# Queries and keys of the differential heads by products of 512 columns, their halves added afterwards

## The chip, the cores and the metric

The kernel runs on one core of a Trainium2 chip. The metric is the device time of one execution in microseconds; 1415.09 us is the median of 3 runs of the kernel before.

## The reference, cut to what matters

The reference is two transformer blocks over 256 tokens of width 1024. The first block normalizes its input, multiplies it by one wide matrix, and splits the result between an RWKV-7 mixer, a differential attention and a gate. The queries and keys of the differential attention are the columns 1792 to 2815 of that product. Cut to them:

```
h = rmsnorm(x, norm_mix_g)                       # (256, 1024)
u = h @ w_in                                     # all projections
q, k, v = split(u_attn, 3)                       # 512 columns each
q = q.reshape(S, 4, 2, 64) * 64 ** -0.5          # factor 0.125
k = k.reshape(S, 4, 2, 64)
s = einsum('qhcd,khcd->hcqk', q, k) - slope * dist, causal
pr = softmax(s);  attn = pr[:, 0] - lam * pr[:, 1];  o = attn @ v
```

## The kernel before, in words

Every projection is computed to full precision from two parts of each factor. The normalized input, still without its factor per token, is held as a high part HH and a low part HL, side by side in one array `h2` (8 slices of 128 features, the two parts, 256 tokens). A weight piece of 2048 columns per partition is loaded (`raw`), ScalarE casts it to its high part (`hi`, L2649), and VectorE subtracts to get the low part (`lo`, L3017). The product is hi·HH + hi·HL + lo·HH, summed in a PSUM bank of 512 columns. Three pieces are in flight, each with its own buffers of `raw`, `hi` and `lo`, and a piece's `hi` is written once TensorE is done with the piece three before it.

The weights of the first block come in pieces of 256 features: seven for the RWKV columns, then four for the queries and keys (columns 1792, 2048, 2304 and 2560; called pieces 1 to 4 here), then the values in wider pieces. Each of the four is a `cols_piece`: for each of two groups of 128 features and each of 8 slices it issues three products of 256 columns (`mm3`, L2131 to L2133), 48 in all, into one bank, one half of the bank for each group. When the bank is full, one VectorE operation multiplies the 512 columns by the factor per token (`RB2`) and, for queries, by 0.125, and writes them to `qT` (L3359) or `kTt` (L3362). That frees the bank.

In the same stretch the RWKV mixer runs: many small products of 64 rows by 64 columns in plain float32 (L2378, L2393), each of which waits for VectorE or ScalarE to have taken the one before from its bank. A planner (`weave`) lays these chains and the wide projections, which it calls fill, into one order for each engine. It keeps estimated times for each engine and always emits the step that could start first; of a `cols_piece` it may break off after every two slices, 0.72 us by its costs. The order is fixed when the program is built. Each engine works through its own list in order, and semaphores hold an instruction until its data is there (`bank_full`, `hi_ready`, `lo_ready`) or its bank is free (`bank_free`). Banks go from a pool of 8, in the order in which they were given back.

The up and gate projections of the later layers already use another form, `wide_runs`: two banks, one for each group of 128 features; a product of 512 columns multiplies `hi` by HH and HL at once (L2219), and one of 256 columns adds lo·HH to the first half of the bank (L2226). That is 16 products of 512 and 16 of 256 columns in one unbroken step. Of such a bank the two halves have to be added afterwards: ScalarE copies the second half out (L2846), and VectorE adds the first half to it (L2987). Every second `wide_runs` begins with one slice of `hi`, then all of `lo`, then the rest of `hi`.

Of the kernel before, what the change touches and what calls it, by code (L numbers as in the profile page):

```python
# [10 lines left out]
ALU = mybir.AluOpType  # L11
# [21 lines left out]
LEAD = 10.0  # L33
# [187 lines left out]
def program(nc, ws, xin, pin, colsin, constin, smallin, rowin, out):  # L221
# [4 lines left out]
    with ExitStack() as ctx:  # L226
# [28 lines left out]
        rstd_ready = Sig(sem("rstd_ready"))  # L255
        factors = Sig(sem("token_factors"))
        diag_ready = Sig(sem("diag_ready"))
        c_part = Sig(sem("c_part"))
        c_ready = Sig(sem("c_ready"))
        rwkv_a = Named(sem("rwkv_act"))  # L260
# [278 lines left out]
        script = []  # L539
# [1063 lines left out]
                state["gates"] = True  # L1603

        def diff():
            while "vd" not in state or "bonus" not in state:
                yield None
            yield "dve"
            emit("lam", dve=0.5, act=0.2, us=state["bonus"], v=diff_v.add(), v_a=diff_a.add())
# [52 lines left out]
                state["ob_v"] = diff_v.n  # L1662
            state["ob"] = pv

        to_shift = []
        early = []

# [14 lines left out]
        def mixers_fill(nm):  # L1682
            for p, c in enumerate(RWKV_ORDER):
                def shift(sl, c, nxt, p=p):
                    early.append((p, c, sl, cur[0]))
                    if p == 1:
                        nm.rows()
                    if p:
                        to_shift.extend(early)
                        early.clear()  # L1690
                    if nxt:
                        emit_lo(nxt)
                    return True
                if p == 0:
                    yield from first_piece(c, nm.h_needs, shift)
                else:
                    yield from cols_piece("w_in", 0, c, "h", nm.h_needs, shift)

            def dq(sl, c, nxt):
                emit("dqk", dve=0.7, slot=sl, n=(c - 1792) // 128)  # L1700
                if nxt:
                    emit_lo(nxt)
                state["dk"] = sl

            for c in range(1792, 2816, 256):
                yield from cols_piece("w_in", 0, c, "h", nm.h_needs, dq)

            def vd(sl, b, h):
                emit("d_v", act=0.7, slot=sl, b=b, rstd=nm.rstd)
                state["dv"] = sl  # L1710

            yield from rows_mat("w_in", 0, 8, 2816, 512, "h", nm.h_needs, vd)
            state["vd"] = True

            def gate_in(g, half):
                def evac(sl, b, h):
                    emit("gate_in", dve=0.7, slot=sl, g=g, b=b, half=half, rstd=nm.rstd)
                    if b:
                        state["g" + g, half] = sl
                return evac  # L1720

            for g, c in (("A", 3328), ("B", 4352)):
                yield "pe"
                while g == "B" and ("fold", 1) not in state:
                    yield None
                for half in range(2):
                    yield from rows_mat("w_in", 0, 8, c + 512 * half, 512, "h", nm.h_needs, gate_in(g, half))
            yield "pe"
            while "ob" not in state or "gates" not in state:
                yield None  # L1730

            def pb(half):
                def evac(sl, b, h):
                    emit("pb", dve=0.7, slot=sl, b=b, half=half, sig=state["sig", "B", half])
                return evac

            for half in range(2):
                if half:

                    yield "pe"  # L1740
                    while "oa" not in state:
                        yield None
                yield from rows_mat("w_proj_b", 0, 4, 512 * half, 512, "ob", lambda k, b: (diff_v.sem, state["ob_v"]),
                                    pb(half))

        weave([shifts(), rwkv_decays(), rwkv_keys(), (rwkv_chain(), LEAD), (rwkv_block(0), LEAD), (rwkv_block(1), LEAD),
               (rwkv_out(0), LEAD), (rwkv_out(1), LEAD), (diff(), LEAD + 2.0), gates()],
              [mixers_fill(nm)])

# [362 lines left out]
        def tensor_program(e):  # L2112
# [27 lines left out]
            for s in script:  # L2140
# [351 lines left out]
                elif kind == "d_soft":  # L2492
# [1 line left out]
                    for z in s["slots"]:  # L2494
                        claim(z)
                    if h == 0:
                        read_out(state["dk"])
                    for a0, a1 in ((0, 128), (128, 384)):
                        for c, z in enumerate(s["slots"]):
                            t = e.matmul(banks[z.b][:, a0:a1], qT[half(c), h, a0:a0 + 128], kTt[half(c), h, 0:a1 - a0],  # L2500
# [97 lines left out]
                elif kind == "pv":  # L2598
# [8 lines left out]
                                         ETb[s["i"]][:, p, c0:c0 + 256 - q0], start=b == 0, stop=b == 1)  # L2607
                    t.then_inc(full[sl.b], 1)

        def scalar_program(e):  # L2610
            own = [0]

# [25 lines left out]
            for s in script:  # L2638
# [51 lines left out]
                                 accum_out=st[:, i:i + 1]).then_inc(x_squared.sem, 1)  # L2690


                elif kind == "shift_old":
                    read_out(sl)
                    c, u_ = s["c"] // 128, ub[s["i"]]
# [253 lines left out]
        def vector_program(e):  # L2949
# [25 lines left out]
            def row_top(sl, bias, E, top):  # L2975
# [2 lines left out]
                                       top[:, 0:1])  # L2978
                return e.tensor_tensor_reduce(E[:, 128:384], banks[sl.b][:, 128:384], bias[:, 128:384], 1.0, LOWEST,
                                              ALU.add, ALU.max, top[:, 1:2])  # L2980

            def add_halves(s, to):

# [39 lines left out]
            for s in script:  # L3023
# [330 lines left out]
                    e.tensor_tensor(obL[:, h, :], oT[:, :], obH[:, h, :].bitcast(F), ALU.subtract).then_inc(diff_v.sem, 1)  # L3354
                elif kind == "dqk":
                    n = s["n"]
                    ready(sl)
                    if n < 4:
                        e.scalar_tensor_tensor(qT[:, n:n + 2, :], b2(sl), 0.125, RB2, ALU.mult,  # L3359
                                               ALU.mult).then_inc(free[sl.b], 1)  # L3360
                    else:
                        e.tensor_tensor(kTt[:, n - 4:n - 2, :], b2(sl), RB2, ALU.mult).then_inc(free[sl.b], 1)  # L3362


                elif kind == "gate_in":
                    b, o = s["b"], slice(512 * s["half"], 512 * s["half"] + 512)
                    e.wait_ge(rstd_ready.sem, s["rstd"])
# [369 lines left out]
```

## Time and profile before

| | |
|---|---|
| median of 3 runs | 1415.09 us (1414.96 to 1415.43) |
| profiled execution | 1415.34 us, of which the span is 1413.4 us |
| TensorE busy | 1406.8 us of the span |
| VectorE, ScalarE busy | 1179.5 us, 819.2 us |
| pieces 1 to 4 begin | about 56.4 us after the span's start |

The profile gives for each group of instructions its line, engine, operation, operands, number, busy time, mean duration of one, and the idle time before them. A matmul's duration in it is longer than the distance to the next one, since matmuls are pipelined: what one costs is read from the start of one to the start of the next. A matmul in plain float32 shows as two records.

### The profile page before, as it was taken

What the parts mean: (1) busy time and instruction counts of PE and PEld (TensorE: products, weight loads), DVE (VectorE), ACT (ScalarE), POOL (GpSimd) and SP (SyncE); (2) the same over time, 40 slices, a digit from 0 to 9 for tenths busy, and PEclk for the clock granted to TensorE, in tenths of its full rate; (3) what the DMA queues carried; (4) which work ended last, traced back from release to release, by engine and by line L of the source; (5) the groups of instructions that cost most, each with busy time, mean ns of one, the idle gap of its engine ahead of it and who ended that gap; (6) DMA issues with size and microseconds to landing.
All of it is one profiled execution on the core that took longest, in us unless ns stands there. A gap on an engine that the chain in (4) does not pass through costs nothing.

```text
span 1413.4 us, 22918 instructions
## 1 busy us (share of the span) xinstructions
PE 1406.8 (100%) x9197; PEld 1197.1 (85%) x9197; DVE 1179.5 (83%) x1641; ACT 819.2 (58%) x1103; POOL 26.5 (2%) x93
## 2 busy tenths in 40 slices
PE   9999999999999999999999999999999999999999
PEld 8988778888888888889878888888888887888887
DVE  6876786898877898998868988988889798688897
ACT  7735474565447555555766665555555557665562
POOL 0000000000001100000000000000000000000000
PEclk9999999999999999999999999999999999999999
DMA  8441236555554555455434555545555453355543
GB/s 335 155 151 62 101 110 208 173 185 203 194 221 179 185 203 185 173 208 192 141 118 172 185 195 187 213 169 197 200 179 197 165 177 148 112 201 195 180 177 119
DMA packets 36105, 249.12 MB, mean 176 GB/s; under 512 B 4128, under 2 KB 4256, under 8 KB 6688
## 3 DMA queue, kind: packets, MB, share of 16 engines
q1 hardware_dynamic: 35712, 247.46, 49.4%
q8 instruction: 74, 1.21, 0.4%
q14 instruction: 31, 0.25, 0.1%
q10 hardware_dynamic: 288, 0.19, 0.1%
HBM read 246.59 MB, written 1.05 MB: 175 GB/s over the span
## 4 chain that ended last, share of the span: by engine, by line
PE 97%; DMA 1%; ACT 1%; DVE 0%; issue 0%; SPq 0%; DVEq 0%; ACTq 0%
PE ps L2219 24%; PE ps L2131 16%; PE ps L2133 15%; PE ps L2132 15%; PE ps L2226 13%; PE ps L2393 2%; PE ps L2203 1%; PE ps L2207 1%; PE ps L2209 1%; DMA raw<-ws 1%; PE ps L2307 1%; PE ps L2606 1%; PE ps L2586 1%; PE ps L2595 1%; PE ps L2378 0%; ACT hi L2649 0%
## 5 line engine op out<-in xcount | busy, mean ns | idle before, releaser
L3017 DVE TENSOR_TENSOR lo<-raw,hi 128x2048 fp32r<-128x2048 f32 (+1 forms) x230 | 525.0, 2283 | 60.3 <-ACT hi L2649 57.6
L2649 ACT CAST hi<-raw 128x2048 fp32r<-128x2048 f32 (+1 forms) x230 | 439.8, 1913 | 186.6 <-PE ps L2133 118.9
L2219 PE MATMUL ps<-h,hi 128*128 128x512 f32 x1504 | 359.0, 390 | 0.0
L2219 PEld LDWEIGHTS ps<-h,hi 128*128 128x128 f32 x1504 | 276.4, 188 | 52.5
L2131 PE MATMUL ps<-hi,a 128*128 128x512 f32 x516 | 205.0, 397 | 0.0
L2133 PE MATMUL ps<-hi,a 128*128 128x512 f32 x516 | 201.4, 390 | 0.0
L2132 PE MATMUL ps<-lo,a 128*128 128x512 f32 x516 | 201.2, 390 | 0.0
L2226 PEld LDWEIGHTS ps<-h,lo 128*128 128x128 f32 x1504 | 192.2, 190 | 7.9
L2226 PE MATMUL ps<-h,lo 128*128 128x256 f32 x1504 | 194.4, 282 | 0.0
L2846 ACT COPY a<-ps 128x256 f32<-128x256 f32 x208 | 76.1, 373 | 143.5 <-PE ps L2219 78.5
L2131 PEld LDWEIGHTS ps<-hi,a 128*128 128x128 f32 x516 | 96.9, 188 | 22.6 <-issue 2.4
L2133 PEld LDWEIGHTS ps<-hi,a 128*128 128x128 f32 x516 | 96.9, 188 | 20.9
L2132 PEld LDWEIGHTS ps<-lo,a 128*128 128x128 f32 x516 | 97.0, 188 | 19.1
L2131 PE MATMUL ps<-hi,h 128*128 128x512 f32 x272 | 112.0, 412 | 0.0
L2133 PE MATMUL ps<-hi,h 128*128 128x512 f32 x272 | 106.3, 391 | 0.0
L2132 PE MATMUL ps<-lo,h 128*128 128x512 f32 x272 | 106.2, 390 | 0.0
L2987 DVE TENSOR_TENSOR a<-ps,a 128x256 f32<-128x256 f32 x208 | 81.9, 420 | 17.0 <-ACT a L2846 15.1
L2131 PE MATMUL ps<-h,hi 128*128 128x256 f32 x224 | 64.8, 289 | 0.9 <-DVE lo L3017 0.9
L2132 PE MATMUL ps<-h,hi 128*128 128x256 f32 x224 | 63.4, 283 | 0.0
L2133 PE MATMUL ps<-h,lo 128*128 128x256 f32 x224 | 63.4, 283 | 0.0
L2131 PEld LDWEIGHTS ps<-hi,h 128*128 128x128 f32 x272 | 51.1, 188 | 12.2 <-issue 2.3
L2133 PEld LDWEIGHTS ps<-hi,h 128*128 128x128 f32 x272 | 51.0, 188 | 11.2
(383 smaller groups left out, 1800.1 us busy)
## 6 DMA issues: line engine op xcount, KB each, us to landing
raw<-ws SPq DMA_DIRECT2D x229, 1024.0 KB, 4.8
X<-xin SPq DMA_DIRECT2D x8, 256.0 KB, 5.3
raw<-ws SPq DMA_DIRECT2D x2, 512.0 KB, 6.5
out<-X SPq DMA_DIRECT2D x4, 256.0 KB, 2.2
small<-small SPq DMA_DIRECT2D x1, 992.5 KB, 12.8
const<-const SPq DMA_DIRECT2D x1, 900.0 KB, 6.8
a<-row SPq DMA_DIRECT2D x1, 512.0 KB, 6.2
const<-const SPq DMA_DIRECT2D x1, 388.0 KB, 13.2
```

The lines of the kernel that those rows point to most:

```text
L2131: e.matmul(o, ah, bh, start=start, stop=False)
L2132: e.matmul(o, ah, bl, start=False, stop=False)
L2133: return e.matmul(o, al, bh, start=False, stop=stop)
L2203: t = e.matmul(b2(sl), wh[:, k, a:a + 128], h2[:, k, :, :], start=k == 0, stop=False)
L2207: t = e.matmul(b2(sl)[:, 0, :], wl[:, k, a:a + 128], HH[:, k, :], start=False, stop=hi_first and k == 7)
L2219: t = e.matmul(b2(s["slots"][u]), wh[:, k, 128 * u:128 * u + 128], h2[:, k, :, :], start=k == 0, stop=last)
L2226: t = e.matmul(b2(s["slots"][u])[:, 0, :], wl[:, k, 128 * u:128 * u + 128], HH[:, k, :], start=False, stop=last)
L2393: t = e.matmul(banks[z.b][half(q ^ n), 64 * h:64 * h + 64], TB[blk][l][half(q), h, :], TB[blk][r][half(q), h, :], start=True, stop=True)
L2649: e.copy(hi[j % NSPL][:, n], raw[j % NRAW][:, n]).then_inc(hi_ready, 1)
L2846: e.copy(half_to[s["to"]][s["j"]][:, s["u"], :], b2(sl)[:, 1, :]).then_inc(half_a.sem, 1)
L2987: e.tensor_tensor(to[:, u, :], b2(x)[:, 0, :], half_to[kind][j][:, u, :], ALU.add).then_inc(free[x.b], 1)
L3017: e.tensor_tensor(lo[j % NSPL][:, n], raw[j % NRAW][:, n], hi[j % NSPL][:, n].bitcast(F), ALU.subtract).then_inc(lo_ready, 1)
```

## The change

The four pieces become `wide_runs`. A new chain in the planner, `queries`, takes the two banks of each piece in turn: a step `halves` on ScalarE copies the second half of both banks into the place in `qT` or `kTt` (two copies of 256 columns), and a step `dqk` on VectorE adds the first half of each (two operations of 256 columns, each of which frees its bank), waits for its own writing, and then multiplies the 512 columns in place by the factor per token (and 0.125). The heads' first score product waits for the last of these. The chain `diff` starts only when `queries` has ended, besides what it waited for before.

```
 def queries():
+    for n in range(4):
+        while len(to_scale) <= n:
+            yield None
+        c, sl, other, at = to_scale[n]
+        yield "act", at
+        emit("halves", act=0.7, slots=(other, sl), qk="dq" if n < 2 else "dk", n=2 * n % 4, v=[half_a.add() for _ in range(2)])
+        halves = script[-1]["v"]
+        yield "dve"
+        emit("dqk", dve=1.4, slots=(other, sl), halves=halves, n=(c - 1792) // 128, v=scaled_v.add())
+        for x in (other, sl):
+            give(x)
+    state["dk"] = scaled_v.n
...
-            def dq(sl, c, nxt):
-                emit("dqk", dve=0.7, slot=sl, n=(c - 1792) // 128)
-                if nxt:
-                    emit_lo(nxt)
-                state["dk"] = sl
+            def dq(sl, c, nxt, other):
+                to_scale.append((c, sl, other, cur[0]))
+                emit_lo(nxt)
+                return True
...
-                yield from cols_piece("w_in", 0, c, "h", nm.h_needs, dq)
+                yield from wide_runs("w_in", 0, c, nm.h_needs, begin, dq)
...
-                        read_out(state["dk"])
+                        e.wait_ge(scaled_v.sem, state["dk"])
...
+                elif kind == "halves":
+                    to = halves_of(s)
+                    for u, x in enumerate(s["slots"]):
+                        ready(x)
+                        e.copy(to[:, u, :], b2(x)[:, 1, :]).then_inc(half_a.sem, 1)
...
+            def meet_halves(s, to):
+                for u, x in enumerate(s["slots"]):
+                    e.wait_ge(half_a.sem, s["halves"][u])
+                    e.tensor_tensor(to[:, u, :], b2(x)[:, 0, :], to[:, u, :], ALU.add).then_inc(free[x.b], 1)
+                for x in s["slots"]:
+                    read_out(x)
+                return to
...
-                    ready(sl)
-                    if n < 4:
-                        e.scalar_tensor_tensor(qT[:, n:n + 2, :], b2(sl), 0.125, RB2, ALU.mult,
-                                               ALU.mult).then_inc(free[sl.b], 1)
-                    else:
-                        e.tensor_tensor(kTt[:, n - 4:n - 2, :], b2(sl), RB2, ALU.mult).then_inc(free[sl.b], 1)
+                    t = meet_halves(s, halves_of({"qk": "dq" if n < 4 else "dk", "n": n % 4}))
+                    t = e.scalar_tensor_tensor(t, t, 0.125 if n < 4 else 1.0, RB2, ALU.mult, ALU.mult)
+                    t.then_inc(scaled_v.sem, 1)
```

The lines move with the edit: what was L2131 to L2133 is L2151 to L2153 in the changed kernel, L2219 and L2226 are L2239 and L2246, the small products L2378 and L2393 are L2398 and L2413, and the cast L2649 is L2673.

On TensorE, around the first score product of the mixer (a_70 by a_71, 64x64), stood before, in the middle of piece 3:

```order
L2131 MATMUL ps<-h,hi_52 128x256
L2132 MATMUL ps<-h,hi_52 128x256
L2133 MATMUL ps<-h,lo_55 128x256
L2378 MATMUL ps<-a_70,a_71 64x64 [waits rwkv_dve,bank_free3,bank_free2]
L2378 MATMUL ps<-a_70,a_71 64x64 x15
L2131 MATMUL ps<-h,hi_52 128x256
L2132 MATMUL ps<-h,hi_52 128x256
L2133 MATMUL ps<-h,lo_55 128x256
```

It now stands between pieces 3 and 4, the second score product behind piece 4:

```order
L2246 MATMUL ps<-h,lo_55 128x256 [waits lo_ready]
L2246 MATMUL ps<-h,lo_55 128x256 x15
L2398 MATMUL ps<-a_70,a_71 64x64 [waits rwkv_dve,bank_free4,bank_free6]
L2398 MATMUL ps<-a_70,a_71 64x64 x15
L2239 MATMUL ps<-h,hi_53 128x512 [waits hi_ready,bank_free0,bank_free7]
L2239 MATMUL ps<-h,hi_53 128x512
L2246 MATMUL ps<-h,lo_56 128x256 [waits lo_ready]
L2246 MATMUL ps<-h,lo_56 128x256 x15
L2239 MATMUL ps<-h,hi_53 128x512 x14
L2398 MATMUL ps<-a_71,a_70 64x64 [waits rwkv_dve,bank_free4,bank_free6]
L2398 MATMUL ps<-a_71,a_70 64x64 x15
```

A piece is no longer broken into, and the small products that lay in four places inside pieces 3 and 4 come between or behind them, closer together. Some rows on, they follow one another through the two banks 4 and 6 (the third score product, then the turning of the values with L2370, between them a chain product L2413), with one to three slices of the value projection between:

```order
L2398 MATMUL ps<-a_70,a_71 64x64 [waits rwkv_dve,bank_free4,bank_free6]
L2398 MATMUL ps<-a_70,a_71 64x64 x15
L2151 MATMUL ps<-hi_54,h 128x512
L2152 MATMUL ps<-lo_57,h 128x512
L2153 MATMUL ps<-hi_54,h 128x512
L2370 MATMUL ps<-const,a_67 128x128 [waits c_ready,bank_free6]
L2370 MATMUL ps<-const,a_67 128x128 x3
L2413 MATMUL ps<-a_86,a_85 64x64 [waits bank_free4]
L2413 MATMUL ps<-a_86,a_85 64x64 x15
L2370 MATMUL ps<-const,a_67 128x128 [waits c_ready,bank_free6]
L2370 MATMUL ps<-const,a_67 128x128 x3
L2151 MATMUL ps<-hi_54,h 128x512 [waits bank_free2,lo_ready]
```

What moved here is the distance: fewer slices of the projection lie between small products that use the same two banks.

On VectorE stood before, from the second query piece (a_101 is `qT`, a_102 is `kTt`) on:

```order
L3359 SCALAR_TENSOR_TENSOR a_101<-ps,RB 128x512 [waits bank_full7]
L3152 SCALAR_TENSOR_TENSOR a_67<-a_69,cols,a_67 128x256 [waits c_part]
L3153 SCALAR_TENSOR_TENSOR a_67<-a_69,cols,a_67 128x256
L3219 TENSOR_TENSOR a_85<-ps,const 128x256 [waits bank_full2,rwkv_dve]
L3219 TENSOR_TENSOR a_85<-ps,const 128x256 [waits bank_full3]
L3017 TENSOR_TENSOR lo_56<-raw_50,hi_53 128x2048 [waits hi_ready,bank_free2]
L3219 TENSOR_TENSOR a_86<-ps,const 128x256 [waits bank_full5,rwkv_dve]
L3219 TENSOR_TENSOR a_87<-ps,const 128x256
L3219 TENSOR_TENSOR a_86<-ps,const 128x256 [waits bank_full6]
L3219 TENSOR_TENSOR a_87<-ps,const 128x256
L3362 TENSOR_TENSOR a_102<-ps,RB 128x512 [waits bank_full1,bank_free5]
L3228 TENSOR_TENSOR a_90<-a_85,const 128x512 [waits bank_free3]
```

and now, from the taking of the first score product on (a_85), up to that of the second (a_86, a_87):

```order
L3257 TENSOR_TENSOR a_85<-ps,const 128x256 [waits bank_full6,rwkv_dve]
L3257 TENSOR_TENSOR a_85<-ps,const 128x256 [waits bank_full4]
L3055 TENSOR_TENSOR lo_57<-raw_51,hi_54 128x2048 [waits hi_ready,bank_free6]
L3015 TENSOR_TENSOR a_101<-ps,a_101 128x256 [waits half_act] x2
L3396 SCALAR_TENSOR_TENSOR a_101<-a_101,RB 128x512 [waits bank_free2,bank_free1]
L3234 TENSOR_TENSOR a_70<-a_67,a_77 128x8x128 [waits rwkv_act,c_ready]
L3235 TENSOR_TENSOR st<-a_77,st 128x4x3
L3240 SCALAR_TENSOR_TENSOR a_80<-a_67,cols 128x256 [waits rwkv_dve]
L3240 SCALAR_TENSOR_TENSOR a_80<-a_67,cols 128x256 x3
L3257 TENSOR_TENSOR a_86<-ps,const 128x256 [waits bank_full6,rwkv_dve]
L3257 TENSOR_TENSOR a_87<-ps,const 128x256
L3257 TENSOR_TENSOR a_86<-ps,const 128x256 [waits bank_full4]
```

One operation per piece has become three, and the second score product is now taken behind the second piece's three and behind four other operations of the mixer.

On ScalarE stood before, between two casts of weights and behind them:

```order
L2649 CAST hi_52<-raw_49 128x2048 [waits bank_full1,raw_in0]
L2696 ACTIVATE a_67<-a_68,st 128x256 [waits bank_free0]
L2697 ACTIVATE a_67<-a_68,st 128x256
L2755 COPY a_88<-ps 128x512 [waits bank_full7]
L2755 COPY a_89<-ps 128x512 [waits bank_full2]
L2649 CAST hi_53<-raw_50 128x2048 [waits bank_full4,raw_in1]
L2747 COPY a_74<-ps 128x512 [waits bank_full0]
```

and now, with the copies of pieces 3 and 4:

```order
L2721 COPY a_102<-ps 128x256 [waits bank_full3]
L2721 COPY a_102<-ps 128x256 [waits bank_full5]
L2673 CAST hi_53<-raw_50 128x2048 [waits bank_full0,raw_in1]
L2776 COPY a_74<-ps 128x512 [waits bank_full6] x2
L2721 COPY a_102<-ps 128x256 [waits bank_full7]
L2721 COPY a_102<-ps 128x256 [waits bank_full0]
L2784 COPY a_88<-ps 128x512 [waits bank_full4]
L2784 COPY a_89<-ps 128x512 [waits bank_full6]
```

The copies of piece 4 stand behind the two that take the turned values (a_74) out of bank 6.

## Rows read from the trace of the kernel before

**Rows 1.** The page: busy time of each engine, granted clock by slices
```profile
PE 1406.8 (100%) x9197; PEld 1197.1 (85%) x9197; DVE 1179.5 (83%) x1641; ACT 819.2 (58%) x1103; POOL 26.5 (2%) x93
...
PEclk9999999999999999999999999999999999999999
```

**Rows 2.** Stretches: us, busy us of PE, PEld, DVE, ACT, POOL; clock, DMA, GB/s
```profile
60.00:80.00 20.00, 20.00 (x252) 19.26 (x252) 16.57 (x20) 7.45 (x7) 0.00 (x0) 1.00 0.30 107
80.00:100.00 20.00, 20.00 (x239) 16.27 (x237) 16.42 (x23) 7.84 (x9) 0.00 (x0) 1.00 0.53 187
```

**Rows 3.** Timeline of TensorE (start, us, what): first products of pieces 1 and 2
```profile
56.37 0.28 PE L2131 MATMUL ps<-h,hi 128*128 128x256 f32 x1
...
62.13 0.28 PE L2131 MATMUL ps<-h,hi 128*128 128x256 f32 x1
```

**Rows 4.** Timeline of TensorE: a piece by `wide_runs` in a later layer
```profile
269.83 4.92 PE L2219 MATMUL ps<-h,hi 128*128 128x512 f32 x21
274.59 2.08 PE L2226 MATMUL ps<-h,lo 128*128 128x256 f32 x16
276.50 0.63 PE L2219 MATMUL ps<-h,hi 128*128 128x512 f32 x2
```

**Rows 5.** Timeline of TensorE: small products inside the projections
```profile
69.21 0.28 PE L2133 MATMUL ps<-h,lo 128*128 128x256 f32 x1
69.42 0.69 PE L2378 MATMUL ps<-a,a 64*64 64x64 f32 x32
70.05 0.39 PE L2131 MATMUL ps<-h,hi 128*128 128x256 f32 x1
70.27 0.28 PE L2132 MATMUL ps<-h,hi 128*128 128x256 f32 x1
...
90.11 1.13 PE L2357 MATMUL ps<-a,const 128*128 128x256 f32 x4
90.89 0.58 PE L2131 MATMUL ps<-hi,h 128*128 128x512 f32 x1
...
93.85 1.03 PE L2357 MATMUL ps<-a,const 128*128 128x256 f32 x4
94.81 1.15 PE L2393 MATMUL ps<-a,a 64*64 64x64 f32 x32
...
99.89 1.16 PE L2393 MATMUL ps<-a,a 64*64 64x64 f32 x64
```

**Rows 6.** Timeline of VectorE over pieces 2 to 4
```profile
62.33 0.69 DVE L3359 SCALAR_TENSOR_TENSOR a<-ps,RB 128x512 f32<-128x512 f32 x1 [2.83 <-PE ps L2133]
...
69.39 0.48 DVE L3152 SCALAR_TENSOR_TENSOR a<-a,cols,a 128x256 f32<-128x256 f32 x1
...
70.24 0.76 DVE L3219 TENSOR_TENSOR a<-ps,const 128x256 f32<-128x256 f32 x2
70.91 2.28 DVE L3017 TENSOR_TENSOR lo<-raw,hi 128x2048 fp32r<-128x2048 f32 x1
73.11 1.41 DVE L3219 TENSOR_TENSOR a<-ps,const 128x256 f32<-128x256 f32 x4
...
76.16 0.68 DVE L3228 TENSOR_TENSOR a<-a,const 128x512 f32<-128x512 f32 x1
...
80.69 1.22 DVE L3196 TENSOR_TENSOR a<-a,a 128x1024 f32<-128x1024 f32 x1
...
82.03 1.68 DVE L3202 SCALAR_TENSOR_TENSOR a<-a,cols 128x256 f32<-128x256 f32 x4
```

**Rows 7.** The page: groups of copies and additions of halves in later layers
```profile
L2846 ACT COPY a<-ps 128x256 f32<-128x256 f32 x208 | 76.1, 373 | 143.5 <-PE ps L2219 78.5
...
L2987 DVE TENSOR_TENSOR a<-ps,a 128x256 f32<-128x256 f32 x208 | 81.9, 420 | 17.0 <-ACT a L2846 15.1
```

**Rows 8.** Groups by line, 260 to 400 us, VectorE: scaling from and to SBUF
```profile
L3396 DVE SCALAR_TENSOR_TENSOR a<-a 128x512 f32<-128x512 f32 x16 | 11.1, 693 | 1.7
```

**Rows 9.** Timeline of ScalarE: copies of the turned values
```profile
86.37 0.59 ACT L2747 COPY a<-ps 128x512 f32<-128x512 f32 x1 [0.62 <-PE ps L2350]
```

More of the change, by code:

```diff
@@ L257, in program @@
         diag_ready = Sig(sem("diag_ready"))
+        scaled_v = Sig(sem("queries_scaled"))
         c_part = Sig(sem("c_part"))
@@ L1605, in diff @@
         def diff():
-            while "vd" not in state or "bonus" not in state:
+            while "vd" not in state or "bonus" not in state or "dk" not in state:
                 yield None
@@ L1663, in diff, with queries @@
             state["ob"] = pv
+        to_scale = []
+        def queries():
+            for n in range(4):
[10 more added lines that the diff above has]
+            state["dk"] = scaled_v.n
         to_shift = []
@@ L1697, in mixers_fill, with begin @@
                     yield from cols_piece("w_in", 0, c, "h", nm.h_needs, shift)
-            def dq(sl, c, nxt):
-                emit("dqk", dve=0.7, slot=sl, n=(c - 1792) // 128)
-                if nxt:
-                    emit_lo(nxt)
-                state["dk"] = sl
+            def dq(sl, c, nxt, other):
+                to_scale.append((c, sl, other, cur[0]))
+                emit_lo(nxt)
+                return True
+            def begin(sl, c, u):
+                pass
             for c in range(1792, 2816, 256):
-                yield from cols_piece("w_in", 0, c, "h", nm.h_needs, dq)
+                yield from wide_runs("w_in", 0, c, nm.h_needs, begin, dq)
             def vd(sl, b, h):
@@ L1744, in mixers_fill @@
                                     pb(half))
-        weave([shifts(), rwkv_decays(), rwkv_keys(), (rwkv_chain(), LEAD), (rwkv_block(0), LEAD), (rwkv_block(1), LEAD),
+        weave([shifts(), queries(), rwkv_decays(), rwkv_keys(), (rwkv_chain(), LEAD), (rwkv_block(0), LEAD), (rwkv_block(1), LEAD),
                (rwkv_out(0), LEAD), (rwkv_out(1), LEAD), (diff(), LEAD + 2.0), gates()],
@@ L2608, in tensor_program, with halves_of @@
                     t.then_inc(full[sl.b], 1)
+        def halves_of(s):
+            return {"dq": qT, "dk": kTt}[s["qk"]][:, s["n"]:s["n"] + 2, :]
         def scalar_program(e):
```

## The prediction

> **What bounds the kernel now.** I read the page first, then the stretches, then TensorE's own timeline, and only then the lists of VectorE and ScalarE. On the page TensorE is busy for 1406.8 of 1413.4 us at a granted clock of 0.9 or more in every slice [rows 1], and from 60 to 100 us, where the four pieces lie, it is busy for all of both stretches, at clock 1.00, which is the level of 2.4 GHz [rows 2]. VectorE is busy there for 16.6 and 16.4 of 20 us, ScalarE for less than 8 [rows 2]. A pipelined TensorE that shows as busy can still lose time, so the reader should look at the starts: piece 1 begins at 56.37 us and piece 2 at 62.13 us [rows 3], 48 products in 5.76 us, 0.120 us each, with nothing lost between them. In this part, then, the end of the program moves by exactly what TensorE's list loses or gains. VectorE waits for it (2.83 us for the end of piece 1 [rows 6]), not the reverse.
>
> **The change part by part.** *The products.* A slice of one group cost three products of 256 columns, 0.360 us. In a later layer 21 products of 512 columns take from 269.83 to 274.59 us, 0.2267 us each, and 16 of 256 take from there to 276.50 us, 0.119 us each [rows 4]. A slice will cost 0.346 us, a piece 16 x 0.346 = 5.54 us instead of 5.76 us. Four pieces save 4 x 0.22 = 0.88 us. The columns streamed are the same, 768 for a slice; what goes is what a product costs beyond its columns: 256 columns more cost 0.2267 - 0.120 = 0.107 us, so each product carries about 0.013 us besides, and 64 products disappear.
>
> The Trainium skill puts this besides-cost lower: TensorE: Matmul & The Clock Gate, section "Back-to-back issue gap", gives a gap of the columns divided by 2.4 GHz plus 2.5 ns. By it the four pieces would save 64 x 2.5 ns = 0.16 us; an estimate from that page, and the trace of this kernel does not agree with it (0.120 us for 256 columns, where the page would have 0.109 us). The sum goes by the rows.
>
> *The small products.* A score product inside a piece costs more than its own time: the product before it takes 0.21 us instead of 0.12 us to its successor, the first one after it 0.22 us instead of 0.12 us [rows 5]; and with an estimated 0.1 us to let the 64x64 block end, one entry and exit is near 0.30 us. Between the start of piece 1 and the first paired chain product (both mixer blocks interleaved) the order has ten such blocks before and seven now, which saves up to 3 x 0.30 = 0.90 us. But inside the merged blocks the shape changes six times instead of three, and such a change costs 0.1 to 0.2 us: 128-row products followed by the projection last 0.78 us (90.11 to 90.89), followed by 64x64 products 0.96 us (93.85 to 94.81) [rows 5]. Three more at 0.15 us take 0.45 us back. I take a saving of 0.45 us, between 0 and 0.90 us.
>
> *VectorE.* Before: four operations of 0.69 us [rows 6], 2.8 us. Now per piece two additions of 0.42 us [rows 7] and one scaling of 0.69 us from SBUF [rows 8], 1.53 us; 6.1 us for four, 3.4 us more. The stretches leave 7 us of VectorE idle between 60 and 100 us [rows 2], and the wait of 2.83 us for piece 1 disappears because the next weight split no longer stands behind the scaling. So most of it is hidden. It is not hidden in one place. By the new order VectorE takes the first score product when piece 3 and that product are done: pieces 1 to 3 end at 56.37 + 3 x 5.54 = 72.99 us, the product about 0.8 us later, its results are read from 73.9 us on. Then follow, before TensorE's third score product can have its two banks: the two takings (0.67 us, 70.24 to 70.91), the split (2.20 us, 70.91 to 73.11) [rows 6], piece 2's additions and scaling with a wait for its own writing (1.4 us from one start to the next), three operations of the mixer (1.34 us, 80.69 to 82.03, then 1.7 us), and the four takings of the second score product (1.41 us) [rows 6]: 8.7 us, so 82.6 us. TensorE, which does piece 4 (5.54 us), the second score product (0.8 us) and three slices of the values (9 x 0.2267 = 2.04 us) in that time, is there at 82.3 us. It loses 0.4 us. The next product, the turning of the values, needs the first bank of the third score product; in between VectorE has two operations of 0.48 us and one of 0.68 us and a taking of 0.42 us [rows 6], until about 84.4 us, against one slice on TensorE until 84.2 us: 0.2 us more. Then the second turning's bank is freed by a ScalarE copy of 0.59 us [rows 9], with one slice (0.68 us) beside it: 0.1 to 0.2 us. Together I take 0.8 us of new waiting, between 0 and 2.5 us: none if VectorE's operations overlap a little better than start to start, 2.5 us if each of its nine operations of pieces 1 to 3 brings 0.2 us of semaphore time with it (1.8 us).
>
> *ScalarE.* Eight copies of 0.37 us [rows 7], 3.0 us, on an engine with 12 us idle in each of the two stretches. The copies of piece 4 stand between the turned values and the outputs of the first chain products; these outputs are late by 0.7 us, and what waits for their banks comes a score product later, so I cost it at nothing; without that cover it would be 0.7 us, inside the bound above.
>
> *What else moves.* The first 512-column products of a piece wait only for the cast and no longer for the split; no wait for a split was seen here, so nothing is gained. A piece holds two banks instead of one; the last two it takes are free 2 us ahead by the same walk. From the first paired chain product on, the orders of all engines are the same but for bank numbers, and VectorE and ScalarE wait for TensorE there in both. DMA queues keep their order.
>
> *The sum.* -0.88 - 0.45 + 0.8 = -0.5 us on the profiled execution of 1415.34 us: 1414.8 us. That execution is 0.25 us above the median of 1415.09 us, so the median I predict is 1414.5 us.
>
> **The rivals.** *A. No new waiting.* The walk along VectorE's list is accurate to a few tenths only, and its first margin is 0.4 us. For it: VectorE gains 2.8 us on its list at piece 1. Against it: the additions stand right before the operations that the second score product waits behind. Time: 1415.09 - 0.88 - 0.45 = 1413.8 us.
>
> *B. The two shared banks decide.* The third score product, the turning of the values and the chain products between go through the banks 4 and 6 one right after the other, and every one of them waits for VectorE or ScalarE to empty the bank. TensorE's distance between them is one to three slices, VectorE's up to 8.7 us. From 1.3 us of waiting on, this eats the whole saving; at the upper bound of 2.5 us the time is 1415.09 - 1.33 + 2.5 = 1416.3 us. If ScalarE's late outputs also hold TensorE, 0.7 us more: 1417.0 us. For it: VectorE's list is filled to 82 percent here already [rows 2]. Against it: after the first paired chain product both lists meet TensorE again, so no delay is passed on.
>
> *C. The saving per product is not there*, because a 512-column product inside the mixer's stretch meets the small ones: with the low bound of all (no gain from the blocks, 0.16 us for the products) and 0.8 us of waiting the time would be 1415.7 us. Against it: the same form holds its 0.2267 us in a later layer [rows 4].
>
> **How the numbers follow.** Forecast (0 to 1.2 us of waiting, saved 0.9 to 1.7 us): 0.60, own range 1413.6 to 1415.3 us. A: 0.15. B: 0.18. C: 0.07. The range that should hold 8 in 10 goes from the full saving of 1.78 us without waiting (1413.3 us) to B without the ScalarE part (1416.3 us); with the runs' spread of half a microsecond I take 1413.0 to 1416.4 us. A run of this kernel tells 0.2 percent, 2.8 us, from no change. Faster by that would need 1412.3 us or less, more than all savings together: 0.04. Slower by it would need 1417.9 us or more, over 4 us of waiting: 0.06. The rest, 0.90, lies within.
>
> **What the changed profile would show.** Starts of pieces 1 and 2 5.54 us apart; the products of 512 and 256 columns at 0.227 and 0.120 us. VectorE's wait of 2.8 us at piece 1 gone. TensorE idle some tenths before the third score product and before the first turning of the values, and nowhere else new up to 100 us; the first paired chain product (99.89 us before [rows 5]) starts at about 99.3 us, and everything behind it half a microsecond early. I am wrong if that product starts later than before, if TensorE waits at piece 4 for its banks, or if anything behind it moves by more than what stands there.

## The result and the profile after

The changed kernel takes 1418.34 us (median of 13 runs, 1417.09 to 1419.58) where the kernel before takes 1415.23 us (13 runs beside them, 1414.93 to 1416.07): 3.1 us more, a ratio of 1.0022 with a 95% interval of 1.0014 to 1.0030. The prediction was 1414.5 us with a range of 1413.0 to 1416.4 us, so it was wrong, and it had given such a slowdown a chance of 0.06. The profiled execution of after has a span of 1416.6 us (1418.44 us by its own time), 3.2 us above that of before.

The page gives no hint of the place: the busy time of TensorE even fell, and the clock is the same, to be held beside [rows 1].

```profile
PE 1406.4 (99%) x9133; PEld 1193.2 (84%) x9133; DVE 1182.0 (83%) x1649; ACT 819.6 (58%) x1111; POOL 26.6 (2%) x93
...
PEclk9999999999999999999999999999999999999999
```

The stretches do (columns as in [rows 2]). Where the four pieces lie, TensorE now lacks 0.27 us. The holes are behind them, in stretches whose code the change does not touch: 0.73 us between 100 and 120 us and 2.12 us between 140 and 160 us, where before was busy for all of the 20 us.

```profile
60.00:80.00 20.00, 20.00 (x148) 17.47 (x147) 17.42 (x20) 8.88 (x13) 0.00 (x0) 1.00 0.36 127
80.00:100.00 20.00, 19.73 (x296) 15.42 (x299) 18.20 (x31) 8.96 (x12) 0.00 (x0) 1.00 0.46 163
100.00:120.00 20.00, 19.27 (x449) 15.96 (x444) 9.39 (x30) 10.80 (x24) 0.00 (x0) 1.00 0.16 58
...
140.00:160.00 20.00, 17.88 (x400) 13.99 (x399) 10.53 (x25) 11.51 (x25) 0.00 (x0) 1.00 0.16 55
```

Now the parts in order. TensorE's timeline of after, the answer to [rows 3, 4]: piece 1 starts at 56.80 us, and after 16 products of 512 and 16 of 256 columns piece 2 starts at 62.36 us. That is 5.56 us for a piece instead of 5.76 us, and 0.228 and 0.119 us for a product.

```profile
56.80 3.82 PE L2239 MATMUL ps<-h,hi 128*128 128x512 f32 x16
60.45 2.08 PE L2246 MATMUL ps<-h,lo 128*128 128x256 f32 x16
62.36 0.63 PE L2239 MATMUL ps<-h,hi 128*128 128x512 f32 x2
```

The small products of after, the answer to [rows 5]: the third score product (83.15 us, with a wait in front of it), the first turning of the values (84.83 us), and the first paired chain product at 99.80 us. Counted from the start of piece 1, that product comes after 43.00 us; before it came after 99.89 - 56.37 = 43.52 us. So up to here the change gains 0.52 us. The very next paired product, at 101.79 us, is cut in two: 56 products, a hole, 8 products. In before the same one was a whole run of 64.

```profile
83.15 0.69 PE L2398 MATMUL ps<-a,a 64*64 64x64 f32 x32 [0.19 <-issue]
...
84.83 0.66 PE L2370 MATMUL ps<-const,a 128*128 128x128 f32 x4
...
99.80 1.16 PE L2413 MATMUL ps<-a,a 64*64 64x64 f32 x64
...
101.79 1.04 PE L2413 MATMUL ps<-a,a 64*64 64x64 f32 x56
103.56 0.34 PE L2413 MATMUL ps<-a,a 64*64 64x64 f32 x8 [0.73 <-issue]
```

The same happens twice more, again in the middle of a run of equal 64x64 products, where no bank and no tile changes:

```profile
139.86 1.05 PE L2413 MATMUL ps<-a,a 64*64 64x64 f32 x56
141.94 0.35 PE L2413 MATMUL ps<-a,a 64*64 64x64 f32 x8 [1.03 <-issue]
...
154.57 0.34 PE L2398 MATMUL ps<-a,a 64*64 64x64 f32 x8
156.00 1.04 PE L2398 MATMUL ps<-a,a 64*64 64x64 f32 x56 [1.09 <-issue]
```

From the last start ahead of a hole to the next start it is 0.95, 1.25 and 1.31 us: 3.5 us, where two such products lie some 0.02 us apart. The waits of TensorE from 40 to 230 us (us in total, times, longest), after first and then all that before has there:

```profile
PE ps L2413 <- issue: 1.8, 2, 1.0
PE ps L2398 <- issue: 1.3, 2, 1.1
PE ps L2334 <- DVE X L3416: 0.3, 1, 0.3
```

```profile
PE ps L2314 <- DVE X L3383: 0.3, 1, 0.3
```

The word "issue" is what to look for: as far as the profile shows, no semaphore, no engine and no DMA of data ended these waits. The word alone proves little, since the 0.19 us before the third score product carry it too, and they turn out below to be VectorE's; it is the place, inside a run of equal products, that rules out a bank or a tile here. The chain of waits of after says it too (start, us, what): at 102.84 us it holds nothing but TensorE's own issuing.

```profile
101.86 0.97 PE ps L2413 x56
102.84 0.73 issue
103.56 0.34 PE ps L2413 x8
```

VectorE's timeline, the answer to [rows 6 to 8]: additions of 0.41 us and scalings of 0.69 us, and no wait in front of them. The four takings of the second score product end at 83.05 us, which is where the prediction's walk had them (82.6 us) once the start of piece 1, 0.43 us later, is counted in; they are some tenths in TensorE's way.

```profile
77.25 0.75 DVE L3015 TENSOR_TENSOR a<-ps,a 128x256 f32<-128x256 f32 x2
78.10 0.69 DVE L3396 SCALAR_TENSOR_TENSOR a<-a,RB 128x512 f32<-128x512 f32 x1
...
81.64 1.41 DVE L3257 TENSOR_TENSOR a<-ps,const 128x256 f32<-128x256 f32 x4
...
84.36 0.75 DVE L3257 TENSOR_TENSOR a<-ps,const 128x256 f32<-128x256 f32 x2
```

ScalarE's eight copies (groups by line, 56 to 100 us) cost what [rows 7] say:

```profile
L2721 ACT COPY a<-ps 128x256 f32<-128x256 f32 x8 | 2.5, 372 | 0.0
```

**What the holes have in common.** If all of TensorE's instructions (weight loads, products and the semaphore instructions between them) are counted in order of their starts, from 0 at the start of the trace, the first one behind each hole has the number 1985, 3777 and 4289. All three are 193 modulo 256. Without the semaphore instructions the remainders differ from hole to hole. The page also has a queue of the kind "instruction":

```profile
q8 instruction: 73, 1.20, 0.3%
```

Its packets have 16,384 bytes, and there are 73 of them; TensorE's 18,777 recorded instructions (9133 loads, 9133 products and 511 semaphore instructions) are 73.3 times 256. I took a packet as a block of 256 instructions of 64 bytes, and its transfer as the fetch of that block. The change takes away 64 products, which is 128 instructions or half a block, so that every end of a block behind the pieces falls at another place in the program. My theory was then: TensorE runs out of instructions where a block is gone through faster than the next one is fetched. A page of the Trainium skill, Runtime: NRT & Kernel Launch, section "Instruction fetch mechanics", has the same blocks of 256 instructions and a fetch of the next while one executes, and calls the cost of a boundary mostly hidden; here three boundaries cost 3.5 us.

### The profile page after: what moved, and what is told of

It is laid out like the page before. It is cut to its first block, busy times and chain, and to the rows that moved or that the text cites. A ratio compares the mean times of both kernels' runs of the same rounds, so it can differ in the third digit from the quotient of the medians.

```text
span 1416.6 us, 22810 instructions
## 1 busy us (share of the span) xinstructions
PE 1406.4 (99%) x9133; PEld 1193.2 (84%) x9133; DVE 1182.0 (83%) x1649; ACT 819.6 (58%) x1111; POOL 26.6 (2%) x93
## 4 chain that ended last, share of the span: by engine, by line
PE 96%; DMA 1%; DVE 1%; ACT 1%; issue 1%; SPq 0%; DVEq 0%; ACTq 0%
PE ps L2239 25%; PE ps L2151 15%; PE ps L2153 15%; PE ps L2152 15%; PE ps L2246 13%; PE ps L2413 2%; PE ps L2223 1%; PE ps L2227 1%; PE ps L2229 1%; DMA raw<-ws 1%; PE ps L2327 1%; PE ps L2626 1%; PE ps L2606 1%; PE ps L2615 1%; ACT hi L2673 0%
## 5 line engine op out<-in xcount | busy, mean ns | idle before, releaser
L2673 ACT CAST hi<-raw 128x2048 fp32r<-128x2048 f32 (+1 forms) x230 | 438.8, 1909 | 185.6 <-PE ps L2153 106.1
L2239 PE MATMUL ps<-h,hi 128*128 128x512 f32 x1568 | 374.6, 390 | 0.0
L2239 PEld LDWEIGHTS ps<-h,hi 128*128 128x128 f32 x1568 | 288.1, 188 | 54.8
L2246 PEld LDWEIGHTS ps<-h,lo 128*128 128x128 f32 x1568 | 200.4, 190 | 8.2
L2151 PE MATMUL ps<-hi,a 128*128 128x512 f32 x516 | 205.0, 397 | 0.0
L2246 PE MATMUL ps<-h,lo 128*128 128x256 f32 x1568 | 202.7, 282 | 0.0
L2153 PE MATMUL ps<-hi,a 128*128 128x512 f32 x516 | 201.4, 390 | 0.0
L2151 PEld LDWEIGHTS ps<-hi,a 128*128 128x128 f32 x516 | 96.9, 188 | 22.4 <-issue 2.4
L2153 PEld LDWEIGHTS ps<-hi,a 128*128 128x128 f32 x516 | 96.9, 188 | 20.9
L2151 PE MATMUL ps<-hi,h 128*128 128x512 f32 x272 | 112.0, 412 | 0.0
L2153 PE MATMUL ps<-hi,h 128*128 128x512 f32 x272 | 106.3, 391 | 0.0
L2151 PEld LDWEIGHTS ps<-hi,h 128*128 128x128 f32 x272 | 51.1, 188 | 12.3 <-issue 2.3
L2153 PEld LDWEIGHTS ps<-hi,h 128*128 128x128 f32 x272 | 51.1, 188 | 11.1
L2690 ACT CAST h<-nt 128x512 fp32r<-128x512 f32 x36 | 22.2, 620 | 64.9 <-DVE nt L3131 64.6
L2152 PEld LDWEIGHTS ps<-lo,h 128*128 128x128 f32 x272 | 51.2, 188 | 8.6
L2151 PE MATMUL ps<-h,hi 128*128 128x256 f32 x160 | 46.3, 289 | 0.8 <-DVE lo L3055 0.8
```

The lines of the kernel that those rows point to most:

```text
L2151: e.matmul(o, ah, bh, start=start, stop=False)
L2152: e.matmul(o, ah, bl, start=False, stop=False)
L2153: return e.matmul(o, al, bh, start=False, stop=stop)
L2239: t = e.matmul(b2(s["slots"][u]), wh[:, k, 128 * u:128 * u + 128], h2[:, k, :, :], start=k == 0, stop=last)
L2246: t = e.matmul(b2(s["slots"][u])[:, 0, :], wl[:, k, 128 * u:128 * u + 128], HH[:, k, :], start=False, stop=last)
L2673: e.copy(hi[j % NSPL][:, n], raw[j % NRAW][:, n]).then_inc(hi_ready, 1)
```

## Experiments

Seven kernels, each timed beside before (1415.25 us, 1414.65 to 1415.92, for the first four; 1415.34 us, 1414.72 to 1416.36, for the other three). The added products stand early in the program, where TensorE waits anyway (for all but the whole block, as it turned out). Each call of the matmul in `pad` makes two products of 64x64 by 16 columns with their weight loads, four instructions; a call of `warm` that is dropped is four as well.

**Block ends moved by half a block, in after.**

```diff
-                        warm(sl, 9, ident, ident)
+                        warm(sl, 4, ident, ident)
+                        pad(sl, 21)
...
+                        if s["i"] == 1:
+                            pad(sl, 16)
                         e.wait_ge(lo_ready, s["i"] + 1)
```

This is 37 x 4 - 5 x 4 = 128 instructions more (later expectations say "148 added products"; it is 148 instructions, less 20).

> The changed kernel with 128 more TensorE instructions at the start, where TensorE waits for its input and for the second weight split anyway: five of the nine warming products replaced by 21 products of 64x64 by 16 columns, and 16 more ahead of the second piece. Nothing else moves, on no engine. Theory F (instruction fetch): the three stops of 0.9 to 1.3 us at TensorE instructions 1985, 3777 and 4289, all 193 modulo 256, come from instruction blocks of 16 KB (256 instructions of 64 bytes) that are not there yet when a dense run of small products reaches a block's end; the change removed 128 instructions in front of them, so 128 put back in front return the ends to where they lay before. F expects no such stop, and 1414.5 to 1415.2 us: the half microsecond that the walk forecast, less 0.2 us for the added products. Theory O (the new order itself: VectorE's longer list, ScalarE's late copies, banks 4 and 6): the order is the same, so 1418 to 1418.6 us.

Measured: 1414.72 us (1414.28 to 1415.21, 11 runs), ratio 0.9996 (0.9987 to 1.0005), span 1412.7 us. All three holes are gone and the paired products are whole again:

```profile
99.32 1.16 PE L2422 MATMUL ps<-a,a 64*64 64x64 f32 x64
...
101.31 1.16 PE L2422 MATMUL ps<-a,a 64*64 64x64 f32 x64
...
102.99 1.16 PE L2422 MATMUL ps<-a,a 64*64 64x64 f32 x64
```

So the changed order itself, its products, banks, copies and additions, does not make the 3.5 us: with the block ends elsewhere it has none of the three holes.

**The same in before**, with the same edit.

> The kernel before, its four pieces as they were, with the same 128 more TensorE instructions at the start. F: behind the four pieces the block ends fall where they fall in the changed kernel, so stops of about 1 us appear at the same three places of the program (the second paired chain product, a chain product some 38 us on, a score product some 14 us further), and the time is 1417.5 to 1419 us. O: nothing of VectorE's, ScalarE's or the banks' order has changed, so 1415.2 to 1415.5 us.

Measured: 1418.15 us (1417.37 to 1419.15, 11 runs), ratio 1.0020 (1.0011 to 1.0029). The kernel before, with nothing but 128 instructions more at its start, has after's loss, in after's places (0.86, 0.43 and 1.35 us, numbers 2241, 4033 and 4545; the middle one smaller than the expected 1 us):

```profile
102.15 1.04 PE L2402 MATMUL ps<-a,a 64*64 64x64 f32 x56
103.84 0.34 PE L2402 MATMUL ps<-a,a 64*64 64x64 f32 x8 [0.65 <-issue]
...
140.14 1.05 PE L2402 MATMUL ps<-a,a 64*64 64x64 f32 x56
141.39 0.35 PE L2402 MATMUL ps<-a,a 64*64 64x64 f32 x8 [0.21 <-issue]
...
154.04 0.34 PE L2387 MATMUL ps<-a,a 64*64 64x64 f32 x8
155.51 0.69 PE L2387 MATMUL ps<-a,a 64*64 64x64 f32 x33 [1.13 <-issue]
```

**A quarter of a block, in after** (only the first pad).

```diff
-                            pad(sl, 16)
```

> The changed kernel with 64 more TensorE instructions at the start (21 small products in place of five warming ones). F: the block ends move by a quarter of a block against both; the stops at the three places go or shrink and others may come, so the time is anything from 1414.5 to 1419 us but each stop of more than 0.5 us again stands at an instruction that is 193 modulo 256. O: 1418 to 1418.6 us, with the stops at the products where they were.

Measured: 1415.28 us (1414.93 to 1415.83, 11 runs), ratio 1.0000 (0.9992 to 1.0009). One hole of 0.50 us, at another place, again at a number that is 193 modulo 256 (2497):

```profile
111.02 0.91 PE L2420 MATMUL ps<-a,a 64*64 64x64 f32 x43
112.21 0.57 PE L2420 MATMUL ps<-a,a 64*64 64x64 f32 x21 [0.29 <-issue]
```

**A whole block, in after.**

```diff
-                            pad(sl, 16)
+                            pad(sl, 48)
```

> The changed kernel with 256 more TensorE instructions at the start, a whole block: a control on the added products themselves. F: the ends lie where they lay in the changed kernel, so its three stops are there again, and the time is that of the changed kernel and up to 0.8 us more for the products that do not fit into the start's waits: 1418.2 to 1419.2 us. If added products as such, and not the position of the block ends, cured the stops, it would be below 1416 us. O: the same as F.

Measured: 1421.3 us (1419.54 to 1421.93, 5 runs), ratio 1.0037 (1.0023 to 1.0051). The three holes are back at after's places in the program (1.22, 0.88 and 1.31 us, numbers 2241, 4033 and 4545, each 256 more than in after; a stop of 0.19 us at number 3521 besides):

```profile
104.94 1.04 PE L2422 MATMUL ps<-a,a 64*64 64x64 f32 x56
106.99 0.34 PE L2422 MATMUL ps<-a,a 64*64 64x64 f32 x8 [1.01 <-issue]
```

The time is above the expected 1418.2 to 1419.2 us, and the first paired product starts at 102.96 us, 3.2 us later than in after. Two things make that. The padding was mis-sized: the 96 added products in one run took 2.98 us, which did not fit into the wait. And right behind them, from 19.14 to 22.55 us, the granted clock of TensorE was 0.50, its level of 1.2 GHz: products of 256 columns start 0.21 us apart there and 0.12 us apart afterwards, some 1.4 us in all (first a stretch, columns as in [rows 2], then the timeline).

```profile
19.14:22.55 3.41, 3.41 (x20) 3.41 (x17) 2.05 (x3) 1.10 (x2) 1.30 (x7) 0.50 0.90 372
```

```profile
16.24 2.98 PE L2164 MATMUL ps<-const 64*64 64x16 f32 x96
...
19.73 0.41 PE L2153 MATMUL ps<-h,lo 128*128 128x256 f32 x1
...
22.77 0.28 PE L2153 MATMUL ps<-h,lo 128*128 128x256 f32 x1
```

The five runs show it too: three, the profiled one among them, took 1421.30 to 1421.93 us at a mean granted clock of 0.999, two took 1419.54 and 1419.63 us at 1.000. The median therefore says little of the padding; the holes are as expected.

**What makes a fetch late.** In after the fetch behind the first hole starts at 101.35 us, 2.4 us after TensorE entered the block before it, while 1 MB of weights runs from 98.17 to 101.88 us; the fetch behind the third starts at 153.73 us, the moment at which another 1 MB has landed. So two weight loads were cut:

```diff
-                    e.dma_start(raw[i][:, :], ws[j + NRAW]).then_inc(raw_in[i], 16)
+                    rows = slice(0, 16 if j + NRAW in (17, 20) else 128)
+                    e.dma_start(raw[i][rows, :], ws[j + NRAW][rows, :]).then_inc(raw_in[i], 16)
```

> The changed kernel with the weight loads of two pieces (those that run from 98.17 to 101.88 us and from 150.09 to 153.73 us) cut to 16 of 128 partitions; it leaves out most of those two pieces' weights. Theory (a fetch of TensorE's instructions that is due while 1 MB of weights is under way starts only when that load ends): the stops at 102.6 us (0.91 to 0.95 us) and at 154.7 us (1.27 to 1.31 us) vanish or fall below 0.3 us, the one at 140.7 us (1.21 to 1.25 us), beside which no load stands, is as before; 2.2 us less in all, about 1416.1 us. Rival (the fetch is late by itself, loads have no part): three stops of the same length at the same places, 1418.3 us.

Measured: 1415.61 us (1414.73 to 1416.20, 11 runs), ratio 1.0001 (0.9992 to 1.0010). Both holes are gone in the profile, as the theory had it: their fetches start 0.14 us before and 1.08 us after the block ahead of them is entered, where it was 2.42 and 3.79 us after it. So is the second (number 3777), against the expectation; it has no load beside it, and yet its fetch came 0.24 us after the block was entered, where it was 1.61 us in after:

```profile
101.62 1.16 PE L2413 MATMUL ps<-a,a 64*64 64x64 f32 x64
...
138.74 1.16 PE L2413 MATMUL ps<-a,a 64*64 64x64 f32 x64
...
152.20 1.16 PE L2398 MATMUL ps<-a,a 64*64 64x64 f32 x64
```

The 11 runs fall into two groups, three at 1414.73 to 1414.76 us (the profiled one, 1414.74, among them) and eight at 1415.29 to 1416.20 us. That would fit a second hole that comes in most runs and not in that one, but the others were not profiled. Since a fetch without a load beside it moved by 1.37 us as well, this run alone does not show that the loads were the cause at the other two.

**VectorE's additions cut**, in after with the block ends moved by half a block.

```diff
-                    e.tensor_tensor(to[:, u, :], b2(x)[:, 0, :], to[:, u, :], ALU.add)...
+                    e.tensor_tensor(to[:, u, 0:2], b2(x)[:, 0, 0:2], to[:, u, 0:2], ALU.add)...
```

> The changed kernel with the 148 added products that move the ends of the instruction blocks by 128, and with VectorE's additions of the halves of the four pieces cut to 2 of 256 columns; it leaves out the adding of the other columns. Theory (the new waits at the third score product, 0.26 us above what such a change of shape takes elsewhere, and at the turnings of the values, 0.25 us, are VectorE's work standing in the way): both go, the first paired chain product starts about 0.5 us sooner, the time is about 1414.2 us against 1414.72 us with the additions. Rival (they are ScalarE's copies or the order of the banks): the waits stay, the time is 1414.7 us.

Measured: 1414.19 us (1413.67 to 1414.49, 11 runs), 0.53 us below the kernel with the additions (1414.72 us). Of the two profiles, first with the additions, then without:

```profile
79.50 0.69 PE L2407 MATMUL ps<-a,a 64*64 64x64 f32 x32
...
82.66 0.69 PE L2407 MATMUL ps<-a,a 64*64 64x64 f32 x32 [0.20 <-issue]
...
84.34 0.66 PE L2379 MATMUL ps<-const,a 128*128 128x128 f32 x4
```

```profile
79.15 0.69 PE L2407 MATMUL ps<-a,a 64*64 64x64 f32 x32
...
82.04 0.69 PE L2407 MATMUL ps<-a,a 64*64 64x64 f32 x32
...
83.47 0.65 PE L2379 MATMUL ps<-const,a 128*128 128x128 f32 x4
```

From the third score product to the turning it is 1.68 us with the additions and 1.43 us without; from the second score product to the third, 3.16 and 2.89 us. Together 0.52 us, which is the whole difference of the medians: these waits are VectorE's additions, and they are all that the additions cost. What the scalings cost this run does not show, since they stay.

**Scaling moved behind the mixer's operations**, to take those waits away without leaving work out.

```diff
-                emit("dqk", dve=1.4, slots=(other, sl), halves=halves, n=..., v=scaled_v.add())
+                emit("dqk", dve=0.7, slots=(other, sl), halves=halves, n=...)
+                late.append((c, other, sl))
+            while "bonus" not in state:
+                yield None
+            for c, other, sl in late:
+                yield "dve"
+                emit("dscale", dve=0.7, slots=(other, sl), n=..., v=scaled_v.add())
```

> The changed kernel with the 148 added products that move the ends of the instruction blocks by 128, and with VectorE's scaling of the pieces as a step of its own after the bonus, so that only the additions stand between a piece's end and the mixer's operations. Theory (VectorE's list makes the waits of some 0.5 us before the first paired chain product, and the ends of the instruction blocks decide the rest): waits before that product fall by 0.2 to 0.5 us, about 1414.3 us, unless an end of a block meets a weight load inside a dense run again, which would show as a stop of 0.9 to 1.3 us at an instruction number of 193 modulo 256, 1415.5 to 1417 us. Rival (stops belong to the dense runs after this change, not to the blocks' ends): three stops of 3.4 us whatever the order, 1418 us.

Measured: 1416.67 us (1416.40 to 1416.91, 11 runs), ratio 1.0009 (1.0000 to 1.0018): no gain. The planner, given smaller costs, put other work in between, two score products stand side by side, and TensorE now waits for VectorE at a turning and at a chain product:

```profile
81.36 0.66 PE L2386 MATMUL ps<-const,a 128*128 128x128 f32 x4 [0.47 <-DVE a L3271]
...
86.16 1.15 PE L2429 MATMUL ps<-a,a 64*64 64x64 f32 x32 [0.21 <-DVE a L3271]
```

The only stop at a block's end between 70 and 182 us is one of 0.26 us (number 4545). The two waits and this stop make 0.94 us, where the kernel takes 1.95 us more than the one with the ends moved alone; TensorE is also busy for 1.3 us more (1408.1 against 1406.8 us on the pages), and what makes that is not shown. The theory's 1414.3 us failed at least because the edit was not one edit: it changed the order.

## Why the prediction was wrong

**The rule that the runs show.** For each block of 256 instructions that TensorE enters between 70 and 182 us, the trace gives the time at which it was entered, the start and the duration of the fetch that goes with it (fetches and blocks are paired in order, one for each; it is taken to bring the next block), and the time at which the block's last instruction starts. There are 143 such blocks in the nine kernels. In 12 the fetch had landed 1.19 us or less before that; in every one of them TensorE stood still until 1.25 to 1.53 us after the landing (stops of 0.19 to 1.35 us). In the other 131 it had landed 1.40 us or more before, and the next instruction starts within 0.23 us, the spacing of products of 512 columns. Counted from the records, in us (+64 and +128 are the kernels with so many instructions more), six of the 12 and two of the three tightest blocks that had no stop at the end:

```
kernel, number    block   fetch starts    fetch   landed ahead   from landing   stop
                  lasts   after entry     takes   of last start  to next start
after      4289    4.75      3.79         0.92        0.04           1.35       1.31
after      3777    3.18      1.61         1.44        0.13           1.38       1.25
after      1985    3.69      2.42         0.97        0.30           1.25       0.95
before+128 2241    3.69      2.25         0.98        0.46           1.32       0.86
after+64   2497    5.24      3.51         0.96        0.77           1.28       0.50
before+128 4033    3.18      0.65         1.43        1.10           1.53       0.43
after+128  2241    3.50      1.13         0.97        1.40           1.42       none
before     2241    3.51      0.77         1.27        1.47           1.49       none
```

So a stop is the fetch's delay, plus its duration, plus some 1.3 us, less the time that TensorE spends in the block. The blocks with a stop are short, 3.2 to 5.2 us, and lie in the mixer's runs of 64x64 products. Before was at the edge (1.47 us) and lost nothing.

**By the prediction's steps.** *The products:* 4 x 0.20 = 0.80 us where 0.88 us stood; right. The 0.16 us that it worked out from the Trainium skill, TensorE: Matmul & The Clock Gate, section "Back-to-back issue gap", are not borne out; that section gives the formula for an isolated product and says that a stream of weight loads and products goes by other figures. *The merged small products:* 0.52 us gained up to the first paired product, with 0.52 us of waiting in it, leaves 0.52 + 0.52 - 0.80 = 0.24 us, a remainder that was not measured by itself; I had 0.45 us, within the bounds of 0 to 0.90 us. (Its six changes of shape inside the merged blocks are five in the timeline of after.) *VectorE's waits:* 0.52 us where 0.8 us stood, at the third score product and the turning, the two first places that it named. (By the walk's own terms TensorE is there at 82.2 us, not 82.3 us; the 0.4 us follow from 82.2 us.) *ScalarE:* nothing, as said: no wait for it is listed from 40 to 230 us. The first paired product was to come 0.6 us early; from the start of piece 1 it comes 0.52 us early. With the block ends moved the kernel takes 1414.72 us, and the forecast was 1414.5 us; that the two lie so close is in part luck, since the misses of 0.08 and 0.21 us in the savings and of 0.28 us in the waits cancel.

*What else moves* is the step that failed: it put everything behind the first paired product at nothing, and the runs showed three stops there, 3.5 us in all. It listed engines, banks and DMA queues and found the same orders behind the first paired product, and it concluded that nothing there could change. It had the number that mattered in its first part, "64 products disappear", and did not ask where in the program the instruction blocks would end without them. The last sentence of the prediction named the sign by which this is seen: something behind that product moved by more than what stands there. The profiled execution adds up: piece 1 starts 0.43 us late (56.80 against 56.37 us, ahead of the change; it is 56.30 us with the moved ends), 0.52 us are gained, three holes cost 3.5 us, 3.4 us in all against 3.2 us measured. None of the three rivals had it; B's time lay closest, by another mechanism.

**What stays open.** What sets the start of a fetch when no weights are under way: over the 143 blocks it came from 2.35 us before to 5.68 us after the block was entered, and up to 3.96 us after it without a transfer of weights beside it (1.61 us at the second hole of after, 3.51 us at the hole of after+64). That weights under way hold it back is not settled by the cut loads, as said. The nine traces together speak for it: 42 of the 143 fetches start while a load of 1 MB is under way or within 0.1 us of its end, and 38 of them start in its last 0.54 us or just behind it, though these loads last 3.1 to 3.8 us; the other four start 2.3 to 4.5 us ahead of the end, all in loads that last over 4.5 us. At the third hole the start of the fetch and the end of the load agree to 0.01 us in after, and so they do in before+128 (153.15 us). The Trainium skill, DMA: Bandwidth & Descriptors, section "Queues, rings and completion order", has each DMA engine take turns between its queues, a whole packet of about 9 to 17 descriptors at a time. A load of 1 MB has 144 records in the trace, 9 for each of 16 engines if they are spread evenly; if a record is one descriptor, a fetch that waits for the end of a load agrees with that. The trace shows neither which engine carries a fetch nor when it was due.

## What to carry to other kernels

When an edit adds or removes instructions on an engine that runs through many short ones, count the instructions: every block end behind the edit moves. Look in the trace for stops inside runs of equal instructions whose releaser is "issue", check whether their numbers agree modulo the block, and see whether a 1 MB load runs while the block before them is executed. Count every instruction of the engine, the semaphore instructions too. Where the numbers agree, judge the edit with the block ends moved (a few dozen harmless instructions in an early wait) before calling it slow: here the same change is 3.1 us slower, or 0.5 us below before and within what can be told from no change, by that alone.

## What was not expected of the hardware

A dense run of 64x64 products uses up its instructions (256 in as little as 3.18 us with a few larger products between) about as fast as they are supplied: 0.88 to 1.62 us for a fetch and, where TensorE stood waiting for it, 1.25 to 1.53 us more until the first of them starts. And a kernel that has holes varied more from run to run (2.5 us over 13 runs of after, 1.1 us over 13 of before); that the fetch's start is what varies there is not shown, with one profile of each.
